# A mixture-of-experts layer and two mixer layers on one core: the second context place of an expert block stands behind the down products

## The reference, cut to what matters

```python
def expert_block(args):
    xe, e = args
    gu = xe @ w_gate_up[e] + b_gate_up[e]
    g = jnp.minimum(gu[:, :D_FF], SWIGLU_LIMIT)
    u = jnp.clip(gu[:, D_FF:], -SWIGLU_LIMIT, SWIGLU_LIMIT)
    act = (u + 1.0) * (g * jax.nn.sigmoid(SWIGLU_ALPHA * g))
    return act @ w_down[e] + b_down[e]
...
hc = modulate(rms_norm_2(xc, mix_pre_g[l]), shc1, scc1)
pc = hc @ w_in[l]
qc = q_heads(pc, q_norm_g[l])
kc, vc = kv_heads(pc[..., K_OFF:GU_OFF], k_norm_g[l])
...
attn_c = gqa_attend(qc.reshape(B, n_ctx, N_KV_HEADS, GQA_GROUP, HEAD_DIM_2), kc, vc)
yc = mixer_merge(pc, attn_c.reshape(B, n_ctx, ATTN_WIDTH), ...)
xc = xc + gc1 * rms_norm_2(yc, mix_post_g[l])
```

## Time and profile before

| | |
|---|---|
| Median of three runs | 3309.13 us |
| Profiled execution: its time, its span | 3309.49 us, 3307.7 us |
| TensorE busy (products, weight loads) | 94%, 55% of the span |
| VectorE, ScalarE busy | 42%, 15% |
| Mean granted TensorE clock | 0.965 |
| Chain that ended last, by engine | PE 81%, DMA 10%, DVE 6%, ACT 2% |
| Expert blocks | about 305 to 1740 us of the span |

### The profile page before, as it was taken

The page is one execution under the profiler, slowest core; times in us unless marked ns, Lnnn a source line. Parts: engine busy times, 40 slices in busy tenths (PEclk is TensorE's granted clock), DMA queues, the critical chain, the costliest instruction groups (busy, mean ns, idle before and its releaser), DMA issues.

```text
span 3307.7 us, 31834 instructions
## 1 busy us (share of the span) xinstructions
PE 3093.0 (94%) x12498; PEld 1808.3 (55%) x12498; DVE 1392.6 (42%) x3330; ACT 484.6 (15%) x972; POOL 26.6 (1%) x37
## 2 busy tenths in 40 slices
PE   5877889998998999999998999989999999999898
PEld 3464335554554555555537757844444487487764
DVE  5754553344666554433322884220000337732201
ACT  1122000011221111010111213111000101221100
POOL 0000000000000000000000000100000000000000
PEclk9858999999999999999998999999999999999999
DMA  8513999887887987898893341322121243223342
GB/s 330 229 52 155 409 413 374 369 369 314 348 347 307 384 350 284 365 375 366 371 382 142 131 149 58 147 76 76 52 101 53 100 151 130 101 91 139 128 153 89
DMA packets 101045, 740.63 MB, mean 224 GB/s; under 512 B 11232, under 2 KB 11616, under 8 KB 12160
## 3 DMA queue, kind: packets, MB, share of 16 engines
q1 hardware_dynamic: 99504, 733.00, 55.5%
q10 hardware_dynamic: 1392, 5.56, 0.5%
HBM read 737.47 MB, written 1.05 MB: 223 GB/s over the span
## 4 chain that ended last, share of the span: by engine, by line
PE 81%; DMA 10%; DVE 6%; ACT 2%; issue 1%; DVEq 0%; SPq 0%; ACTq 0%
PE ps L495 26%; PE ps L507 17%; DMA ring<-stream 9%; PE ps L742 9%; PE ps L657 8%; PE ps L822 5%; PE ps L653 3%; PE ps L769 2%; PE ps L757 2%; PE ps L525 2%; DVE area L1031 1%; PE ps L749 1%; PE ps L809 1%; DMA area<-modulation 1%; PE ps L947 1%
## 5 line engine op out<-in xcount | busy, mean ns | idle before, releaser
L495 PE MATMUL ps<-area,ring 128*128 128x256 f32 (+1 forms) x3456 | 865.5, 413 | 0.3
L495 PEld LDWEIGHTS ps<-area,ring 128*128 128x128 f32 x3456 | 662.3, 192 | 200.9 <-issue 122.7
L507 PE MATMUL ps<-ring,area 128*128 128x512 f32 x1440 | 620.7, 593 | 2.5 <-DMA ring<-stream 2.5
L742 PE MATMUL ps<-ring,area 128*64 128x512 f32 x2112 | 486.7, 606 | 34.7 <-DMA ring<-stream 33.4
L507 PEld LDWEIGHTS ps<-ring,area 128*128 128x128 f32 x1440 | 273.6, 190 | 341.6 <-issue 336.4
L742 PEld LDWEIGHTS ps<-ring,area 128*64 128x64 f32 x2112 | 144.5, 139 | 353.0 <-issue 261.3
L1315 DVE SCALAR_TENSOR_TENSOR area<-area,cond 128x256 f32<-128x256 f32 x672 | 269.9, 477 | 0.0
L657 PE MATMUL ps<-area,ring 128*128 128x256 f32 x1152 | 256.4, 381 | 1.8 <-issue 1.1
L822 PE MATMUL ps<-ring,area 128*64 128x512 f32 x1056 | 239.0, 606 | 4.4 <-ACT area L2047 4.4
L657 PEld LDWEIGHTS ps<-area,ring 128*128 128x128 f32 x1152 | 216.9, 190 | 43.5 <-issue 15.8
L1828 DVE TENSOR_TENSOR area<-area 128x512 f32<-128x512 f32 (+1 forms) x64 | 35.8, 559 | 460.6 <-ACT area L2205 460.6
(11 more groups left out here) (305 smaller groups left out, 2035.7 us busy)
## 6 DMA issues: line engine op xcount, KB each, us to landing
ring<-stream SPq DMA_DIRECT2D x626, 1024.0 KB, 8.9
area<-shared_modulation SPq DMA_DIRECT2D x48, 1024.0 KB, 7.0
area<-modulation SPq DMA_DIRECT2D x16, 1536.0 KB, 7.7
x<-x_tiles ACTq DMA_DIRECT2D x1, 1024.0 KB, 12.8
area<-ctx_tiles ACTq DMA_DIRECT2D x1, 1024.0 KB, 4.7
out<-x SPq DMA_DIRECT2D x1, 1024.0 KB, 3.9
cst<-constants ACTq DMA_DIRECT2D x1, 912.5 KB, 14.5
rows<-row_vectors ACTq DMA_DIRECT2D x1, 912.0 KB, 9.4
```

The source lines that it names most:

```text
L495: i = mm(ps[:, b, 0:n], w[:, k % 4, j * P:(j + 1) * P], rhs(k), start=(k == 0), stop=(k == 4 * kgs - 1))
L507: i = mm(ps[:, b, :], lhs(k, t), w[:, k % 4, :], start=(k == 0), stop=(k == 4 * kgs - 1))
L742: i = mm(ps[half(h), bank, :], xT[:, k % 4, half(k // 4)], w[:, 2 * (k % 2) + h, :], start=(k == 0), stop=False)
```

## The change

The heavy step of place B moves behind the down products on TensorE and behind the copy of their result on ScalarE, and its chunk moves behind chunk 11 in the plan and in SyncE's list. VectorE's list is not touched, nor is place l3, which stays last.

```diff
@@ _plan
-            if ci in (4, 8) and (e, "AB"[ci // 8]) in PLACE:
-                step = PLACE[e, "AB"[ci // 8]]
+            if ci == 4 and (e, "A") in PLACE:
+                step = PLACE[e, "A"]
                 put(("cx", step), 1, CX + HEAVY.index(step))
             put(("moe", e, ci), 1, DRAM["moe"] + (e * CPE if e < NE else 0) + ci)
+        if (e, "B") in PLACE:
+            step = PLACE[e, "B"]
+            put(("cx", step), 1, CX + HEAVY.index(step))
@@ TensorE, expert
                 work("l2")
-                work("B")
                 pe.wait_ge(*at((tag, "actT")))
...
                         i.then_inc(*mark("weights_used", (tag, "chunk", 8 + k // 2)))
+                work("B")
                 work("l3")
@@ SyncE
-                    if ci == 8:
+                    one(CH["moe", e, ci], DRAM["moe", e, ci] if e < NE else top * CPE + (DRAM["moe"] + ci))
+                    if ci == CPE - 1:
                         context(e, "B")
-                    one(CH["moe", e, ci], DRAM["moe", e, ci] if e < NE else top * CPE + (DRAM["moe"] + ci))
```

## The result

The changed kernel takes 3343.6 us (median of 4 runs, 3343.19 to 3344.68), the kernel before 3308.07 us (4 runs beside it): a ratio of 1.0107, 95% interval 1.0094 to 1.012. The profiled execution took 3343.19 us, its span is 3341.4, the mean granted clock 0.961 (before 0.965). Forecast were 3339 us and slower.

A forecast was written before the change was run, and what follows sets the result against it. TensorE's own order of work was taken as the bound, with the weight stream close behind. Six terms, (a) to (f), summed to +29.7 on 3309.5 us, giving 3339.2 and a median of 3339, range 3316 to 3358.

The forecast's parts named there:

- (a): Down products, blocks 5 to 30: the hidden block's copy in front of them loses its cover; +16.4 us.
- (b): Blocks 9, 10, 11: the turn straight behind B waits for its chain, stop and lost clock 6.25 us each; +18.8 us.
- (c): Block 24: l3 waits 3.7 us for VectorE's diagonals from B, plus half a turn's clock loss; +4.5 us.
- (d): VectorE reaches the next block's bias row later, short by some 0.3 us in blocks 12 to 15; +1.4 us.
- (e): Block 30: normalisation behind the last output product delays the next block's bias row; +3.3 us.
- (f): Weight stream, blocks 6 to 30: chunks are asked for earlier, gate waits go, block 23's long wait stays; -14.7 us.
- stream decides: Rival: the weight stream bounds the stretch, new stops fall where chunks would be waited for; faster, 3301 us; chance 0.06.
- VectorE decides: Rival: late taps and modulation parts in blocks 10 to 21 stop TensorE, +24, 3363 us; chance 0.12.
- it cancels: Rival: stream gain at its upper bound, no clock lost, copies mostly covered; +9 or none, about 3312 us; chance 0.06.

The follow-up runs named there:

- experiment 3: Changed kernel, but down products read the input tokens instead of the hidden block, with the copy's wait behind them: 3324.55 us, ratio 1.0049.
- experiment 1: Changed kernel, but in blocks 9, 10 and 11 place B and its chunk stand ahead of the down products as before: 3324.66 us, ratio 1.0054.
- experiment 5: Changed kernel, but all convolution taps of a block stand in front of B's vector work on VectorE: 3342.28 us, ratio 1.0102.
- experiment 6: Kernel before (B ahead), with five places in the ring of weights instead of six: 3385.14 us, ratio 1.0228.
- experiment 7: Changed kernel (B behind), with five places in the ring of weights instead of six: 3349.96 us, ratio 1.0122.
- experiment 9: Kernel before, with the block's end reordered: hidden block's transposes and copy first, selection's transposes, its copy and modulation sums behind: 3321.83 us, ratio 1.0039.
- Experiment 4: Changed kernel with 34 useless identity transposes before the wait of each of three turns in blocks 9, 10 and 11: 3336.8 us, ratio 1.0087.
- experiment 2: Changed kernel, but in blocks 9, 10, 11, 24 and 30 place B and its chunk stand ahead of the down products: 3315.5 us, ratio 1.0016.
- experiment 8: Changed kernel with B ahead in blocks 9, 10, 11, 24 and 30, and the hidden block transposed and copied first at each block's end: 3318.08 us, ratio 1.0023.

## Why the prediction was right

The forecast sum was +29.7; the medians say +35.5, the lag table +33.3 over the stretch (34.74 - 1.45). A further 1.45 came ahead of block 5 (1.35 at block 0 already), where nothing was changed. The mechanism held term by term: the path is TensorE's order, and every wait named was there. Some of the sizes were not, and part of the closeness is luck, as the last item says.

- **(a) Copy, +16.4.** Right. 20 waits for L2050 where "about 20 blocks" were forecast. A block without l2 cost 1.05 instead of 0.94, since the width changes twice and not once; 14 such blocks make 14.7. The part that is the wait comes to 11.9 us between block 5 and block 31 by experiment 3's trace, without block 23's slow pass.
- **(b) Turns, +18.8.** Right: experiment 1 gives 18.9. The stops are (20.4 - 8.5)/3 = 4.0 each, 0.2 less than forecast. The clock took more than the 1.65 each: the gates of blocks 10 to 12 take 8.61, 9.39 and 8.61, so 1.7, 2.5 and 1.7 over 6.92, and the up products of blocks 11 and 12 take 0.3 and 1.0 more than before: 7.2 in all, against 5.0. Only one of the three turns had slow transposes. About +1 in all: from block 9 to 13 the lag grew by 20.0, where (a), (b) and (f) make 19.
- **(c) Block 24, +4.5.** The stop is 3.69 as forecast. The step that failed is "I add half of (b)'s 1.65": the 3.7 us stop cost as much clock as the longer ones, a pass of 8.62. From block 24 to 26 the lag grew by 6.25, and the terms make 5.2.
- **(d) Bias rows, +1.4.** Slightly low: the gate passes of blocks 13 to 16 are 7.4 instead of 6.92, 2 us together; in experiment 5's trace all four are 6.92.
- **(e) Block 30, +3.3.** The wait is 3.16, but the lag grew by 5.95 over block 31, since what followed ran slow: the four bias products (1.90 from start to start instead of 0.96), the scatter (2.01 instead of 1.06) and the up pass (7.94 instead of 7.27). This clock was not in the sum: +2.7.
- **(f) Stream, -14.7.** Right: the waits for chunks that made the gates' excess of 13.7 us are gone, and block 23's wait stayed, 6.6 (L745 in all 6.6, where about 8 were forecast). Block 32's gate and up passes give 1.7 back where 1 was forecast. Experiments 6 and 7 show that the order decides it, with an effect about five times as large.
- **Not forecast:** block 23's down products take 1384.13 - 1375.64 = 8.49 us instead of 6.92, at a clock of 0.78, with nothing but small products and a wait of 0.69 ahead; 0.1 of it is the change of width, in (a):

```profile
1372.61 1.84 PE L812 MATMUL ps<-cst,area 128*128 128x1 f32 x16
1374.32 0.64 PE L817 MATMUL ps<-cst,area 128*128 128x128 f32 x4
1375.64 6.85 PE L824 MATMUL ps<-ring,area 128*64 128x512 f32 x24 [0.69 <-ACT area L2050]
...
1384.13 7.17 PE L660 MATMUL ps<-area,ring 128*128 128x256 f32 x32
```

- **Luck.** Block 32's down products take 9.46 us in the profile of the kernel before and 7.79 after, and 7.78 to 7.83 in every other trace of this document. The edit does not touch them. That one slow pass before makes the profile's difference 1.7 us smaller.

So against the forecast stand +1.5 of block 23, +1 of (b), +1.1 of (c) and +2.7 of (e), and on the other side 0.7 of (f) and the 1.7 of luck: +3.9, where 33.3 exceeds 29.7 by 3.6. Nearly all of it is clock.

Of the rivals, *stream decides* fell: the waits for chunks went as it says, and the stops added in full. By the rule of the Trainium skill ("Perfetto Trace Analysis", "Identifying the Most-Contended Engine"), to optimize the most-contended engine first, the stream was to be helped. (The section judges DMA by its HBM utilization; the prediction took the engines' busy share, 0.95.) TensorE's waits for the stream fell from 16.5 to 6.6 us, and the time rose by 1.07%. *VectorE decides* fell by experiment 5, *it cancels* by the ratio (its sum is +9, so 3318; the 3312 that the prediction names needs one more wait gone).

## What to carry to other kernels

A filler between a producer and its reader hides the latency of every pair it stands between: before moving one, list what it covered (here a copy of 1.3 us in 26 blocks, and a 4 us chain in three) and what comes to stand straight behind it. The same holds for banks: the reordering of experiment 9 hid one copy and made the sums wait for another, 0.27 us in 26 blocks. Price a stop of TensorE at its length and at the slower products behind it, read from the traces of your own kernel: here stops of 3.2 to 4.3 us cost 1.1 to 2.9 us more, and filling three of them gave 8.9 us back. Decide such an order block by block: here a kernel with eight blocks in the new order and eighteen in the old one is the fastest. Which of the eighteen lose by the new one is shown only for the three with a turn, together, and for blocks 24 and 30, together.

## Not expected of the hardware

- A stop of 3.7 us cost as much clock behind it (8.62 for a pass of 6.92) as stops of 4.0 and 4.3; one of 3.16 cost 2.6 us. The Trainium skill, "TensorE: Matmul & The Clock Gate", Part 1 (the HAM clock gate), says that the clock follows how busy the engine was recently. Experiment 4 agrees (1.7 us regained in the pass shown).
- Block 23 lost 1.47 behind gaps of 0.7 us at most; before, with B in that place, the clock there was 1.00. The traces of experiments 1, 2, 4, 5 and 7 have this slow pass too (8.49 to 8.60); that of experiment 3, without the wait for the copy, has 7.02:

```profile
1365.59 0.64 PE L817 MATMUL ps<-cst,area 128*128 128x128 f32 x4
1366.15 7.09 PE L823 MATMUL ps<-ring,area 128*64 128x512 f32 x32
```

- The wait is not all of it. In blocks 5 to 30 of all traces of this document, 17 down passes take 8.3 to 8.7 us, one to four in a trace, none in experiment 3's. All 17 are in blocks with B behind; four are in experiment 8's, where the wait is gone. In the three kernels with B ahead everywhere (before, experiments 6 and 9) there is none. So B behind cost some clock without any long stop. What sets it off, and in which block, is open.
